# Delta rule scan in transposed orientation: key matrix, decay and scores built as their transposes

## What is computed

```python
gc = jnp.cumsum(g, axis=-1)
decay = jnp.exp(jnp.where(incl, gc[..., :, None] - gc[..., None, :], -jnp.inf))
kk = jnp.einsum("nbhid,nbhjd->nbhij", k, k)
a_mat = jnp.where(strict, beta[..., :, None] * kk * decay, 0.0) + jnp.eye(CHUNK)
rhs = jnp.concatenate([v * beta[..., None], k * (beta * jnp.exp(gc))[..., None]], axis=-1)
sol = lax.linalg.triangular_solve(a_mat, rhs, lower=True, unit_diagonal=True)   # u, w
qk = jnp.einsum("nbhid,nbhjd->nbhij", q, k) * decay
# scan over chunks, state s:
v_new = u_c - w_c @ s ;  o = (q * exp(gc)) @ s + qk_c @ v_new
s = s * a_last + (k * exp(gc_last - gc)).T @ v_new
```

## Time and profile before

| | us |
|---|---|
| median of 3 runs | 3809.71 (3807.51 to 3811.71) |
| the profiled execution | 3811.74 |
| its span | 3808.7 |
| chunk stage, head group 0 / scan | ends at about 250 / 250 to 439 |
| chunk stage, head group 1 / scan | 439 to 558 / 558 to 749 |

### The profile page before, as it was taken

The page is one execution under the profiler, slowest core; times in us unless marked ns, Lnnn a source line. Parts: engine busy times, 40 slices in busy tenths (PEclk is TensorE's granted clock), DMA queues, the critical chain, the costliest instruction groups (busy, mean ns, idle before and its releaser), DMA issues.

```text
span 3808.7 us, 59782 instructions
## 1 busy us (share of the span) xinstructions
PE 3634.1 (95%) x25058; PEld 2927.4 (77%) x25058; DVE 1942.3 (51%) x3021; ACT 1526.3 (40%) x2602; POOL 821.8 (22%) x807
## 2 busy tenths in 40 slices
PE   6989899999999999999999999999999899999999
PEld 4678778878887667767887788875778688878887
DVE  5656566655355556643344443446565523354343
ACT  4543333333233456643234322235664522343222
POOL 1022222212021224522101121113354211002020
PEclk7999999999999999999999999999999999999999
DMA  6410120022222111112223223220211122322232
GB/s 224 140 49 4 28 63 4 30 105 94 96 99 83 56 50 62 56 45 78 99 100 105 88 95 99 96 74 26 78 62 62 39 97 97 116 84 94 94 100 89
DMA packets 81971, 300.80 MB, mean 79 GB/s; under 512 B 8872, under 2 KB 10024, under 8 KB 81064
## 3 DMA queue, kind: packets, MB, share of 16 engines
q1 hardware_dynamic: 80672, 294.90, 22.9%
q10 hardware_dynamic: 1032, 2.10, 0.5%
HBM read 292.76 MB, written 4.19 MB: 78 GB/s over the span
## 4 chain that ended last, share of the span: by engine, by line
PE 72%; DVE 12%; ACT 6%; issue 5%; POOL 4%; DMA 1%; SPq 0%; DVEq 0%; POOLq 0%; ACTq 0%
PE ps L208 71%; DVE ac L247 2%; DVE wlo L239 1%; DVE he L247 1%; ACT whi L227 1%; PE ps L213 1%; DVE hc L2528 1%; ACT ha L227 1%; POOL p L243 1%; DVE ss L247 1%; ACT L227 1%; DVE ha L239 1%; DVE ws L247 1%; ACT sg L227 1%; ACT wp L228 1%
## 5 line engine op out<-in xcount | busy, mean ns | idle before, releaser
L239 DVE TENSOR_TENSOR wlo<-wraw,whi 128x1024 fp32r<-128x1024 f32 x537 | 691.5, 1293 | 736.2 <-ACT whi L227 735.4
L208 PE MATMUL ps<-hh,whi 128*128 128x512 f32 x1856 | 736.3, 397 | 8.5 <-ACT hh L227 2.2
L208 PE MATMUL ps<-hl,whi 128*128 128x512 f32 x1856 | 727.3, 392 | 0.0
L208 PE MATMUL ps<-hh,wlo 128*128 128x512 f32 x1856 | 727.1, 392 | 0.0
L227 ACT ACTIVATE whi<-wraw 128x1024 fp32r<-128x1024 f32 x537 | 559.6, 1050 | 212.6 <-PE ps L208 175.2
L208 PEld LDWEIGHTS ps<-hh,whi 128*128 128x128 f32 x1856 | 351.3, 189 | 93.4 <-ACT hh L227 7.9
L208 PEld LDWEIGHTS ps<-hh,wlo 128*128 128x128 f32 x1856 | 351.1, 189 | 74.5
L208 PEld LDWEIGHTS ps<-hl,whi 128*128 128x128 f32 x1856 | 351.5, 189 | 70.8
L208 PE MATMUL ps<-u,u 64*64 64x64 f32 (+1 forms) x6016 | 222.4, 226 | 23.6 <-DVE u L239 16.9
L208 PEld LDWEIGHTS ps<-u,u 64*64 64x64 f32 x6016 | 202.5, 134 | 42.7 <-DVE u L239 18.9
L208 PE MATMUL ps<-gh,wlo 128*128 128x512 f32 x528 | 205.4, 389 | 0.0
(11 more groups left out here) (415 smaller groups left out, 6870.7 us busy)
## 6 DMA issues: line engine op xcount, KB each, us to landing
wraw<-weights SPq DMA_DIRECT2D x537, 512.0 KB, 3.3
x<-xT SPq DMA_DIRECT2D x1, 2048.0 KB, 12.3
bias_lines<-ln ACTq DMA_DIRECT2D x1, 2048.0 KB
x<-xT SPq DMA_DIRECT2D x4, 512.0 KB, 5.3
xmf<-memT SPq DMA_DIRECT2D x2, 1024.0 KB, 5.3
out<-x SPq DMA_DIRECT2D x4, 512.0 KB, 2.6
bias<-bias_lines SPq DMA_DIRECT2D x1, 1536.0 KB, 8.6
con<-consts SPq DMA_DIRECT2D x1, 1379.0 KB, 17.1
```

Of the source, the lines that this page charges most:

```text
L208: self.last, self.open = self.e.matmul(out, lhsT, rhs, start=start, stop=stop, skip_group_check=skip), True
L239: return self.e.tensor_tensor(out, a, b, op)
```

## The change

The decay matrix, the key matrix and the scores are computed as their transposes, so that what PE needs as the stationary operand is there at once. One of the two transposes at the start of a unit's inversion remains: the mask is now applied to the transpose, which gives Y, and X is made from it by a transpose (`x0`), which has a phase of its own. Phase `tr` has no PE and no ACT work any more, `pt` is gone, `y0` is gone from `ax` 1. A latent unit has 18 phases as before, a context unit one more than before. Beta scales columns instead of rows: v is scaled by the norm (`kinv`) instead of beta, and beta with the squared norm goes into E and into the decay to the end. For that the key norms are done differently: DVE writes the sums with EPS into `kroot` at k3 step 1 in 8 instructions, and POOL raises all 48 to the power -0.5 and makes the four multiplications, at k3 step 1 too. The constants shrink by 128 columns.

```diff
 def gdn_phases(s):
-    out = ["ga", "kk"] + ["qk"] * (s >= 4) + ["tr"] + ["pt"] * (s >= 4)
+    out = ["ga", "kk"] + ["qk"] * (s >= 4) + ["tr", "x0"]
...
# dve_chunks
             elif kind == "k":
...
                 if i == 3:
-                    dve.wait_ge([dve.at("ksum", hg, j) for j in range(4)])
-                    dve.ts(K.ksum, K.ksum, 1.0, ALU.mult, EPS, ALU.add).then_inc(dve("keps", hg), 1)
-            if (kind, i, step) == ("v", 2, 0):
-                K.dve_key_norms(hg)
+                    K.dve_key_norms(hg)
# pool_chunks
             elif (kind, i) == ("k", 3):
-                pool.wait_ge(K.dve.at("keps", hg))
-                pool.tt(K.ksum, K.ksum, K.con("mhalf").unsqueeze(2).broadcast_to([128, 6, 4]), ALU.pow).then_inc(pool("kroot", hg), 1)
+                K.pool_key_norms(hg)
# dve_key_norms
-                    dve.cp(K.kroot[r, par, lo:hi, :], tiles).then_inc(dve("kroot", hg), 1)
-        beta, nbe, betak = (x[:, :, :, heads] for x in (K.beta, K.nbe, K.betak))
-        dve.wait_ge(dve.at("kroot", hg))
-        dve.tt(beta, beta, K.kroot, ALU.mult).then_inc(dve("kbeta", hg), 1)
-        dve.tt(nbe, nbe, K.kroot, ALU.mult).then_inc(dve("knbe0", hg), 1)
-        dve.wait_ge(dve.at("knbe0", hg))
-        dve.tt(betak, beta, K.kroot, ALU.mult).then_inc(dve("kbetak", hg), 1)
-        dve.tt(nbe, nbe, K.kroot, ALU.mult).then_inc(dve("knbe", hg), 1)
+                    dve.ts(K.kroot[r, par, lo:hi, :], tiles, EPS, ALU.add).then_inc(dve("keps", hg), 1)
+
+    def pool_key_norms(self, hg):
+        K, pool = self, self.pool
+        beta, after, kinv = (x[:, :, :, hg * 4:hg * 4 + 4] for x in (K.beta, K.ex[:, 1], K.kinv))
+        pool.wait_ge(K.dve.at("keps", hg), K.dve.at("nbe"), K.act.at("beta"), K.act.at("ex"))
+        power = K.con("mhalf").unsqueeze(2).unsqueeze(3).broadcast_to([128, 2, 6, 4])
+        pool.tt(kinv, K.kroot, power, ALU.pow).then_inc(pool("kr", hg), 1)
+        pool.wait_ge(pool.at("kr", hg))
+        pool.tt(beta, beta, kinv, ALU.mult).then_inc(pool("kb0", hg), 1)
+        pool.wait_ge(pool.at("kb0", hg))
+        pool.tt(beta, beta, kinv, ALU.mult).then_inc(pool("kb", hg), 1)
+        pool.wait_ge(pool.at("kb", hg))
+        pool.tt(after, after, beta, ALU.mult).then_inc(pool("kafter", hg), 1)
+        pool.tt(kinv, kinv, K.kroot, ALU.mult).then_inc(pool("kinv", hg), 1)
# pe_scan
             elif ph == "tr":
                 if s == 0:
                     K.pe_keep(3, "ramp", hg)
-                b = K.ps.take(pe, "at", *z)
-                pe.wait_ge(dve.at("a", *z))
+            elif ph == "x0":
+                b = K.ps.take(pe, "x0", *z)
+                pe.wait_ge(dve.at("xy", *z, 0))
                 for h in hs:
                     for r in rows:
-                        pe.mm(Q(b, h)[r, :], Q(A, h)[r, :], id_[r, r])
-                pe.mark("at", *z)
-            elif ph == "pt":
-                b = K.ps.take(pe, "pt", *z)
-                pe.wait_ge(dve.at("p", *z))
-                for h in hs:
-                    for r in rows:
-                        pe.mm(Q(b, h)[r, :], Q(PP, h)[r, :], id_[r, r])
-                pe.mark("pt", *z)
+                        pe.mm(Q(b, h)[r, :], Q(Y, h)[r, :], id_[r, r])
+                pe.mark("x0", *z)
             elif ph[0] == "ax":
                 lv = ph[1]
                 b = K.ps.take(pe, "ax", *z, lv)
-                pe.wait_ge(act.at("at", *z), dve.at("xy", *z, lv - 1))
+                pe.wait_ge(act.at("x0", *z), dve.at("xy", *z, lv - 1))
...
-                if lv == 1:
-                    b = K.ps.take(pe, "y0", *z)
-                    for h in hs:
-                        for r in rows:
-                            pe.mm(Q(b, h)[r, :], Q(X, h)[r, :], id_[r, r])
-                    pe.mark("y0", *z)
# act_scan
-            elif ph == "tr":
-                act.wait_ge(pe.at("at", *z))
-                act.cp(BA[:, 256:512], K.ps[("at", *z)][:, 0:256]).then_inc(act("at", *z), 1)
...
+            elif ph == "x0":
+                act.wait_ge(pe.at("x0", *z))
+                act.cp(XY[:, 0:256], K.ps[("x0", *z)][:, 0:256]).then_inc(act("x0", *z), 1)
...
# dve_scan
             elif ph == "tr":
-                X = XY[:, 0:256]
-                dve.wait_ge(pool.at("x0", *z))
-                dve.tt(q4(X), q4(X), bc4(K.con("id64")), ALU.add).then_inc(dve("xy", *z, 0), 1)
+                Y = XY[:, 256:512]
+                dve.wait_ge(pool.at("y0", *z))
+                dve.tt(q4(Y), q4(Y), bc4(K.con("id64")), ALU.add).then_inc(dve("xy", *z, 0), 1)
# pool_scan
             elif ph == "tr":
-                pool.wait_ge(dve.at("a", *z), pe.at("kk", *z))
-                pool.tt(q4(X), q4(A), bc4(K.lvl[:, par, :]), ALU.mult).then_inc(pool("x0", *z), 1)
+                pool.wait_ge(dve.at("a", *z))
+                pool.tt(q4(Y), q4(AT), bc4(K.lvl[:, 1 - par, :]), ALU.mult).then_inc(pool("y0", *z), 1)
```

More of the change, by code:

```diff
@@ L48, in const_table @@
         add(f"aft{par}", pair & np.where(down, r > c, r < c))
-        add(f"strict{par}", np.where(down[:, 0:64], r % 64 > c64, r % 64 < c64))
-        add(f"keep{par}", np.where(down[:, 0:64], r % 64 >= c64, r % 64 <= c64))
+        add(f"upto{par}", np.where(down[:, 0:64], r % 64 <= c64, r % 64 >= c64))
     add("id64", r % 64 == c64)
@@ L495, in layout @@
         self.kroot = self.sb("kroot", G + 408, [128, 2, 6, 4])
-        self.betak = self.sb("betak", G + 480, [128, 2, 6, 8])
+        self.kinv = self.sb("kinv", G + 480, [128, 2, 6, 8])
         self.qsum = self.sb("qsum", G + 976, [128, 4, 4])
@@ L1112, in dve_decay_sums @@
         dve.wait_ge(K.act.at("ex"), K.act.at("beta"))
-        dve.stt(fl(K.nbe), fl(K.ex[:, 0]), -1.0, ALU.mult, fl(K.beta), ALU.mult).then_inc(dve("nbe"), 1)
+        dve.ts(fl(K.nbe), fl(K.ex[:, 0]), -1.0, ALU.mult).then_inc(dve("nbe"), 1)
     def wkey(self, col):
@@ L1335, in dve_key_norms @@
         K, dve = self, self.dve
-        heads = slice(hg * 4, hg * 4 + 4)
-        dve.wait_ge(K.pool.at("kroot", hg), dve.at("nbe"), K.act.at("beta"))
+        dve.wait_ge([dve.at("ksum", hg, i) for i in range(4)], K.pool.at("kb", 0) if hg else None)
         for half in range(2):
@@ L1380, in pe_scan @@
             par, lat, (XY, BA, EP, EQ, R) = K.unit(s)
-            z, inc, pair = (hg, s), K.con(f"inc{par}"), K.pair(s)
-            X, Y, A, AT, E, PP = XY[:, 0:256], XY[:, 256:512], BA[:, 0:256], BA[:, 256:512], EP[:, 0:256], EP[:, 256:512]
+            z, pair = (hg, s), K.pair(s)
+            X, Y, AT, E, PT = XY[:, 0:256], XY[:, 256:512], BA[:, 0:256], EP[:, 0:256], EP[:, 256:512]
             tok = [slice(c * 64, c * 64 + 64) for _, _, c in pair]
@@ L1389, in pe_scan @@
                 pe.wait_ge(pool.at("ga", *z))
-                pe.mm(b[:, 256:512], inc, X)
+                pe.mm(b[:, 256:512], K.con(f"aft{par}"), X)
                 pe.mark("kk", *z)
@@ L1395, in pe_scan @@
                     for d, hf, c in pair:
-                        pe.mm(Q(b, h)[rows[hf], :], K.QT[:, h, (c - 4) * 64:(c - 3) * 64], K.KT[:, h, tok[d]])
+                        pe.mm(Q(b, h)[rows[hf], :], K.KT[:, h, tok[d]], K.QT[:, h, (c - 4) * 64:(c - 3) * 64])
                 pe.mark("qk", *z)
@@ L1430, in pe_scan @@
                 b = K.ps.take(pe, "xy", *z, lv)
-                pe.wait_ge(dve.at("ev", *z, lv), act.at("y0", *z))
+                pe.wait_ge(dve.at("ev", *z, lv))
                 for h in hs if lv < 5 else ():
@@ L1468, in pe_scan @@
                     b = K.ps.take(pe, "o", *z)
-                    pe.wait_ge(act.at("vn", *z), act.at("pt", *z))
+                    pe.wait_ge(act.at("vn", *z), dve.at("p", *z))
                     for h in hs:
                         for r in rows:
-                            pe.mm(H(b, h)[r, :], Q(PP, h)[r, :], H(BA, h)[r, :])
+                            pe.mm(H(b, h)[r, :], Q(PT, h)[r, :], H(BA, h)[r, :])
                     pe.mark("o", *z)
@@ L1509, in act_scan @@
                     v, o = K.VM[r, c // 2, h * 128:h * 128 + 128], R[r, h * 128:h * 128 + 128]
-                    act.a(o, v, ACT.Copy, scale=K.col(K.beta, s, hg, h)[r]).then_inc(act("bv", *z), 1)
+                    act.a(o, v, ACT.Copy, scale=K.col(K.kinv, s, hg, h)[r]).then_inc(act("bv", *z), 1)
             elif ph == "vn":
@@ L1557, in dve_scan @@
                 w = slice(0 if lv < 5 else 256, 512)
-                dve.wait_ge(pe.at("xy", *z, lv), dve.at("xy", *z, lv - 1), act.at("y0", *z))
+                dve.wait_ge(pe.at("xy", *z, lv), dve.at("xy", *z, lv - 1), act.at("x0", *z))
                 dve.tt(XY[:, w], XY[:, w], K.ps[("xy", *z, lv)][:, w], ALU.add).then_inc(dve("xy", *z, lv), 1)
@@ L1598, in pool_scan @@
             z = (hg, s)
-            X, A, E = XY[:, 0:256], BA[:, 0:256], EP[:, 0:256]
+            X, Y, AT, E, PT = XY[:, 0:256], XY[:, 256:512], BA[:, 0:256], EP[:, 0:256], EP[:, 256:512]
             if ph == "ga":
                 pool.wait_ge(K.slot_free(z))
```

(10 more changed lines are left out.)

20 lines of the change are left out of this document (6 added, 14 removed).

## The result

| | us |
|---|---|
| before, median of 20 runs | 3810.07 (3799.99 to 3819.09) |
| changed, median of 20 runs | 3816.34 (3810.24 to 3828.41) |
| ratio changed / before | 1.0020, 95% interval 1.0012 to 1.0027 |
| the profiled execution of the changed kernel | 3810.37 |
| its span | 3808.6 |

The change costs 7.6 us (0.20%; by the interval 4.6 to 10.3). The profiled execution lies 6 us under its own median: it reached the last key sums of head group 0 at 213.97 us, the one of before at 220.38. This point moves from execution to execution: in the profiles of the experiments it lies between 212.74 and 219.21. So the profiles are compared stage by stage, never by absolute times. Helpers stand one line lower in the changed file (L207, L226, L238, L242, L246).

A forecast was written before the change was run, and what follows sets the result against it. PE, busy for 95% of the span, was taken as the bound. Scans -14.2 us and key norms +14.4 made +0.2 on the median of 3809.7, so 3810, range 3799 to 3820.

The forecast's parts named there:

- No change that can be told: Verdict for the whole kernel: two effects of about 14 us cancel, within 0.2% (7.6 us); chance 0.60.
- Part 1: PE groups removed from each scan, priced by place for units 4 to 11: 5.7 us gained a scan.
- The gaps behind `out` of units 2 and 3: Sign in the changed profile: PE's waits for DVE there grow by half a microsecond.
- Counting all 20 groups: All removed `at` and `y0` groups of units 4 to 11 at 0.53 us each: 10.6 us a scan.
- Units 9 and 10: `x0` in `out` turns waits for POOL and DVE: unit 9 loses 0.2 us, unit 10 gains 0.6.
- Part 2: Ramp of each scan, units 0 to 3: gain 1.4 us, bounds 0 and 2.0.
- Part 4: Key norms delay `cm` and PE's v1 transposes: 5.2 us plus 2.0 for the clock, 7.2 lost a chunk stage.
- The clock: After its wait for v1, PE runs at half clock: 2.0 us a chunk stage, bounds 0 and 3.4.
- A: Slower: POOL's queue at k3 is longer, strided products 1.0 us each, 11.6 us lost a stage, 3819; chance 0.14.
- A2: Slower: DVE and POOL set the pace, scans gain only 3 us each, 3818; chance 0.08.
- B: Faster: the power on POOL is mostly fixed cost, PE loses 0.7 us a stage, 3797; chance 0.06.
- C: Faster: removed groups count nearly in full (-20), half clock costs nothing (+10.4), 3800; chance 0.12.

The follow-up runs named there:

- experiment 9: Changed kernel plus a spare, unread group of 16 PE products in `tr` of units 5, 6, 9 and 10, in `out` turns; run once, 3812.79 us.
- experiment 10: Changed kernel plus a spare, unread group of 16 PE products in `tr` of units 4, 7, 8 and 11, ahead of `out` turns; run once, 3815.93 us.
- experiment 6: New scan with key norms as before (products on DVE), POOL doing `tr` of the youngest unit before `out` of the oldest; 3795.69 us, ratio 0.9961 to before.
- experiment 7: Changed kernel with its own key norms, POOL doing `tr` of the youngest unit before `out` of the oldest; 3815.77 us, ratio 1.0011 to before.
- experiment 3: Changed kernel plus seven spare PE products ahead of the transposes of v1; 3809.13 us, ratio 1.0002 to before.
- experiment 2: Kernel before, with its old scan but the new key norms on POOL ahead of `cm` of v1; 3831.32 us, ratio 1.0054 to before.
- experiment 4: Changed kernel with the four key-norm products moved to DVE, the power of 48 left on POOL; 3813.76 us, ratio 1.0014 to before.

## Why the prediction was nearly right, point by point

The forecast was 3810, +0.2 us; measured was 3816, +7.6, inside the range of 3799 to 3820. That two effects work against each other, and where they lie, held. The two sizes were off, both to the slow side: 11.5 us gained (at full clock) instead of 14.2, 19.7 lost instead of 14.4. "No change that can be told" was partly luck: the ratio is 0.20%, just the limit that the prediction had named, and its interval shows a loss.

- **Part 1, by place: the mechanism held.** The intervals of the table gained 0.83, 0.48, 0.38, 1.03, 0.94, -0.41, 0.56 and 1.03 us, against 1.05, 0.57, 0.57, 1.05, 1.05, -0.2, 0.6 and 1.05: 4.8 instead of 5.7. Experiments 9 and 10 show both rules, nothing in the turn of an `out` and about half a microsecond elsewhere. The gaps behind `out` of units 2 and 3 grew from 0.58 to 1.14 and from 0.85 to 1.40, as foretold. Counting all 20 groups would have given 10.6.
- **Units 9 and 10: seen, and a little short.** `x0` waits 0.78 and 0.20 us for POOL and DVE. The place and the cause were right (experiments 6 and 7 remove them by POOL's order alone).
- **Part 2, the ramp: 0.9 instead of 1.4.** Experiment 3 has the ramp at full clock: `kk` of unit 4 comes 38.66 us after `kk` of unit 0, before it was 39.58. `kk` of 3 to `kk` of 4 took 10.91, as walked forward; half a microsecond was lost up to `kk` of 3 (27.75 us after `kk` of 0; the walk gave 27.27). Together 5.8 us a scan at full clock, and experiment 3's first scan is 183.35 long, 189.12 less 5.8.
- **Part 4, the term that was mis-sized.** From the last key sums to v1's transposes it took 10.02 us before (220.38 to 230.40) and 17.41 now (213.97 to 231.38): +7.4, where the forecast had 5.2. The power took 9.03 (forecast 9.5). The term that was too small is the four products: from the start of the first at 224.97 to the start of `cm` at 228.70 it is 3.7 us, where the forecast took 1.8 from the nearest row, 128x16 at 0.39. The second is `cm`, kept at the 1.87 of the earlier trace rows, which takes 2.62. -0.4 + 1.9 + 0.75 = 2.25, which is the difference. What both left out is DVE: at this place its instructions for a weight tile and for the convolution of v2 run beside POOL's, and each of these five POOL instructions ends a fixed time after one of them (the rows are in the last section). The clock cost 2.3 and 2.7 us (forecast 2.0).
- **A stage thus costs 10.** 7.3 + 2.7 in the second stage of the changed kernel, and 10.3 in experiment 2 by the time. In the first stage of the profile PE's wait is 1 us shorter, since PE itself ended v2's projection 10.85 us after the last key sums (213.97 to 224.82), before 9.65 (220.38 to 230.03); from key sums to `kk` it is 9.7 all the same.
- **Rivals.** A (11.6 a stage) had nearly the right size for the products (0.93 us each against its 1.0), but not shown is its reason, the strided form: they wait for DVE. A power of 9.0 and not 10.1 kept the stage under the 10.9 from which it decides; the slopes that the prediction names, 0.16 to 0.20 from 24 elements on, give 8.9 to 9.9, not 10.1. A2 is refuted: the scans gained 5.8 at full clock, not 3. B is refuted by the power, 5.06 us for 24 elements and 9.03 for 48. C is refuted on both halves by experiments 3 and 9.
- **The sum with the measured sizes**: -11.1 + 19.7 = +8.6 in the profiles, against +7.6 (4.6 to 10.3) by the time.

## What to carry to other kernels

The worth of a removed instruction is its pace where its engine runs through and nothing where the engine then waits for another: a spare copy of the group put back at each place measures this directly. Work moved to an idle engine is priced by what stands behind it in that engine's queue: here the same POOL instructions cost 20 us ahead of `cm` of v1 and 14 us less one and two places later. When moved work slides onto a busy stretch of a neighbour, both must be priced again: a mean duration from other places, 0.39, was no price for POOL beside a busy DVE. Before calling an instruction slow, look whether its end follows the neighbour's instructions.

## What the runs showed of the hardware that wasn't expected

- **POOL's products end when DVE's instructions do.** The rows of the first stage of the changed kernel one by one, each DVE instruction with the POOL instruction that runs beside it (`wlo` is the low part of a weight tile):

```profile
224.57 1.22 DVE L238 TENSOR_TENSOR wlo<-wraw,whi 128x1024 fp32r<-128x1024 f32 x1 [2.75 <-ACT whi L226]
224.97 0.96 POOL L238 TENSOR_TENSOR beta<-beta,kinv 128x48 f32<-128x48 f32 x1
225.86 0.62 DVE L242 TENSOR_SCALAR ac<-zb,vec 128x772 f32<-128x772 f32 x1
226.01 0.61 POOL L238 TENSOR_TENSOR beta<-beta,kinv 128x48 f32<-128x48 f32 x1
226.52 1.02 DVE L246 SCALAR_TENSOR_TENSOR ac<-zb,vec,ac 128x772 f32<-128x772 f32 x1
226.70 0.98 POOL L238 TENSOR_TENSOR ex<-ex,beta 128x48 f32<-128x48 f32 x1
227.57 1.02 DVE L246 SCALAR_TENSOR_TENSOR ac<-zb,vec,ac 128x772 f32<-128x772 f32 x1
227.65 1.09 POOL L238 TENSOR_TENSOR kinv<-kinv,kroot 128x48 f32<-128x48 f32 x1
```

The four products end at 225.94, 226.62, 227.68 and 228.74, each 0.14 us after a DVE instruction. So do all 56 products in the profiles of the seven kernels that have them on POOL (0.14 to 0.15 us), whether they took 0.48 or 1.10. Their durations are mostly waits; no run shows what such a product costs beside an idle DVE. The row that the prediction priced them by shows the same: of its 32 products of 128x16, those that meet no DVE instruction took 0.21 to 0.22 us, those that start while over 0.5 us of a `wlo` is left took 0.64 to 0.90 and end 0.1 us or less after it, and 0.39 is the mean of all. One that waited:

```profile
1416.85 1.22 DVE L239 TENSOR_TENSOR wlo<-wraw,whi 128x1024 fp32r<-128x1024 f32 x1
1417.28 0.87 POOL L239 TENSOR_TENSOR dec<-dec 128x16 f32<-128x16 f32 x1 [49.49 <-ACT dec L227]
```

On DVE in experiment 4 the four products took 0.20 to 0.23. It works the other way too: in the kernel before, one such product on DVE met `cm` and ended 0.07 us after it:

```profile
237.33 1.84 DVE L239 TENSOR_TENSOR betak<-beta,kroot 128x48 f32<-128x48 f32 x1
```

- **`cm` and DVE's instructions wait for each other in the same way.** `cm`, 2.62 us long, ends 1.67 after the third step of DVE's convolution (228.63 to 229.65), and the fourth step, begun at 229.69, takes 2.45 instead of 1.02 and ends 0.82 after `cm`. In experiment 4 `cm` ends 1.67 after DVE's `wlo` (224.84 to 226.06), and the first step of the convolution takes 2.17 instead of 0.62, ending 0.42 after `cm`. This is read from the traces of all runs; no experiment moved DVE's work away to test it.
- **The power on POOL grows with its elements**: 5.06, 6.35 and 9.03 us for 24, 32 and 48 a partition, 0.17 us for each of the last 24. All of these started during a `wlo` of DVE. Powers of 4 elements took 1.01 us alone and 1.93 to 1.96 when started so, so 0.9 us of each may be the wait. The 1.13 of the earlier trace rows is a mean of both kinds.
- **The power does not hold DVE up.** DVE's convolution of v1 ran beside the 9.03 us at its full pace:

```profile
217.62 4.20 DVE L246 SCALAR_TENSOR_TENSOR ac<-zb,vec,ac 128x772 f32<-128x772 f32 x4
```

The Trainium skill, "SBUF — State Buffer", section "SBUF: two separate sides", says that VectorE operations with two SBUF inputs or in a 2-port mode, and GpSimd operations, take one port pair in turns, each holding it for a whole instruction. The products, `cm` and the steps that waited for it agree with that, if the one-input step (0.62 us where a two-input one takes 1.02) is in such a mode, which no run here shows. The undisturbed 4.20 beside the long power is not what it would give; there the measurement decides, and why the power is different stays open.
